# Reading the weight stream of an f32 transformer kernel two 1 MB blocks per transfer

## The reference

```
mod = silu(c) @ ada_w + ada_b            # 2048 -> 6144: shift, scale, gate
h   = rmsnorm(x) * (1 + scale) + shift
u   = h @ w_in                           # 2048 -> 16 heads q, k, v, z; 32 heads q, k, v, z; two gates
o_a = gated_delta_rule(silu(conv(qkv_a)), g, beta)      # 16 heads, chunks of 64
o_b = swa_with_sinks(rope(q_b), rope(k_b), v_b)         # 32 query heads, window 128
y   = sigmoid(g_a) * (o_a @ proj_a) + sigmoid(g_b) * (o_b @ proj_b)
x   = x + gate * (y @ w_out)
# third layer: neighborhood attention, a two-way linear recurrence, a gated feed-forward
# (2048 -> 5632 -> 2048), and a gated embedding product, each with its norms
```

## Time and profile before

| | |
|---|---|
| median of 3 executions | 4971.2 us (4965.88 to 4974.19) |
| the profiled execution | 4966.8 us, span 4965.0 us |
| TensorE busy | 4319.7 us, 87% of the span |
| VectorE busy | 2718.9 us, 55% |
| ScalarE busy | 2001.3 us, 40% |
| GpSimd busy | 222.4 us, 4% |
| HBM read | 752.64 MB, 152 GB/s over the span |
| mean granted TensorE clock | 0.927 |

### The profile page before, as it was taken

The page is one execution under the profiler, slowest core; times in us unless marked ns, Lnnn a source line. Parts: engine busy times, 40 slices in busy tenths (PEclk is TensorE's granted clock), DMA queues, the critical chain, the costliest instruction groups (busy, mean ns, idle before and its releaser), DMA issues.

```text
span 4965.0 us, 85375 instructions
## 1 busy us (share of the span) xinstructions
PE 4319.7 (87%) x33128; PEld 4146.8 (84%) x33128; DVE 2718.9 (55%) x3528; ACT 2001.3 (40%) x2916; POOL 222.4 (4%) x188
## 2 busy tenths in 40 slices
PE   2989898899979989898979997998996799999968
PEld 2888787799869988887869986997895799999958
DVE  7455655465657645556546565764345454555444
ACT  2333434244433434334324343334345444444443
POOL 0011111000000001111110000000000000000000
PEclk8999999699989989999969998998998899999979
DMA  8422222274348733222217532873332344444522
GB/s 352 141 97 103 98 103 102 93 279 153 122 147 298 247 110 120 97 101 98 105 54 264 203 119 101 298 257 136 112 138 85 127 166 174 171 176 173 186 96 102
DMA packets 117707, 757.57 MB, mean 153 GB/s; under 512 B 13008, under 2 KB 13328, under 8 KB 35600
## 3 DMA queue, kind: packets, MB, share of 16 engines
q1 hardware_dynamic: 87984, 639.17, 35.5%
q10 hardware_dynamic: 29536, 115.68, 6.7%
HBM read 752.64 MB, written 2.16 MB: 152 GB/s over the span
## 4 chain that ended last, share of the span: by engine, by line
PE 73%; DVE 9%; ACT 7%; issue 6%; DMA 2%; ACTq 1%; DVEq 1%; POOL 0%; SPq 0%; POOLq 0%
PE bank L275 17%; PE bank L276 17%; PE bank L277 17%; PE bank L779 2%; PE bank L740 2%; PE bank L1728 1%; PE bank L1730 1%; PE bank L1729 1%; PE bank L783 1%; DVE Wl L291 1%; DMA raw<-in_ada 1%; DVE WS L531 1%; PE bank L728 1%; ACT Wh L285 1%; PE bank L757 1%
## 5 line engine op out<-in xcount | busy, mean ns | idle before, releaser
L275 PE MATMUL bank<-Hh,Wh 128*128 128x256 f32 x7232 | 2129.8, 294 | 92.9 <-DVE Hl L410 34.4
L285 ACT CAST Wh<-raw 128x1024 fp32r<-128x1024 f32 x1140 | 1186.8, 1047 | 2332.5 <-PE bank L277 1875.0
L276 PE MATMUL bank<-Hl,Wh 128*128 128x256 f32 x7232 | 2067.9, 286 | 0.0
L277 PE MATMUL bank<-Hh,Wl 128*128 128x256 f32 x7232 | 2065.5, 286 | 0.0
L291 DVE TENSOR_TENSOR Wl<-raw,Wh 128x1024 fp32r<-128x1024 f32 x1140 | 1390.1, 1229 | 1214.1 <-ACT Wh L285 1211.4
L275 PEld LDWEIGHTS bank<-Hh,Wh 128*128 128x128 f32 x7232 | 1411.9, 195 | 139.5 <-issue 88.9
L276 PEld LDWEIGHTS bank<-Hl,Wh 128*128 128x128 f32 x7232 | 1411.9, 195 | 13.2 <-issue 12.6
L277 PEld LDWEIGHTS bank<-Hh,Wl 128*128 128x128 f32 x7232 | 1408.8, 195 | 0.0
L275 PE MATMUL bank<-Oh,Wh 128*128 128x256 f32 x1024 | 289.8, 283 | 0.0
L276 PE MATMUL bank<-Ol,Wh 128*128 128x256 f32 x1024 | 289.8, 283 | 0.0
L277 PE MATMUL bank<-Oh,Wl 128*128 128x256 f32 x1024 | 289.7, 283 | 0.0
(11 more groups left out here) (311 smaller groups left out, 4818.5 us busy)
## 6 DMA issues: line engine op xcount, KB each, us to landing
raw<-in_stream SPq DMA_DIRECT2D x572, 1024.0 KB, 4.8
gm_more<-in_ada ACTq DMA_DIRECT2D x80, 512.0 KB, 5.2
raw<-in_ada SPq DMA_DIRECT2D x32, 1024.0 KB, 7.5
WS<-in_ada ACTq DMA_DIRECT2D x48, 512.0 KB, 4.6
WS<-in_ada ACTq DMA_DIRECT2D x16, 1024.0 KB, 4.9
gm_more<-in_ada ACTq DMA_DIRECT2D x16, 1024.0 KB, 8.1
WS<-rows_d ACTq DMA_DIRECT2D x16, 512.0 KB, 5.9
X<-in_x_t SPq DMA_DIRECT2D x1, 2048.0 KB, 17.0
```

The costliest lines, as they stand in the source:

```text
L275: pe.matmul(out[:, 0:T], wh, xh[:, kt, :], start=first, stop=False)
L276: pe.matmul(out[:, 0:T], wh, xl[:, kt, :], start=False, stop=False)
L277: mm = pe.matmul(out[:, 0:T], wl, xh[:, kt, :], start=False, stop=last)
L285: act.copy(Wh[:, n % 4, :], raw[:, (sbk + 2) % 4, k * (D // 2):(k + 1) * (D // 2)]).then_inc(hi_ready, 1)
```

## The change

A read now fetches two neighbouring blocks into two neighbouring slots (2 MB), and there is one semaphore for each pair of slots. The read of blocks b and b+1 waits for what the read of block b+1 alone waited for. In the loop it is `lo_ready` of at least 2b-4; at the start it is the `ada` slab that freed the second slot. The casts of both blocks wait for the pair's semaphore. The number of reads falls from 572 to 286.

```diff
-        landed = [sem(f"raw{i}_landed") for i in range(4)]
+        landed = [sem(f"raw_pair{i}_landed") for i in range(2)]
...
         def act_cast(act, q, sbk, k):
 
             n = 2 * sbk + 4 + k
-            act.wait_ge(landed[(sbk + 2) % 4], (q + ((sbk + 2) // 4 + 1)) * 16)
+            act.wait_ge(landed[(sbk + 2) % 4 // 2], (q + ((sbk + 2) // 4 + 1)) * 16)
...
-            for s in range(4):
-                sp.wait_ge(ada_used, 2 * KT - 3 + s)
-                sp.dma_start(raw[:, s, :], stream[s]).then_inc(landed[s], 16)
+            for s in range(0, 4, 2):
+                sp.wait_ge(ada_used, 2 * KT - 2 + s)
+                sp.dma_start(raw[:, s:s + 2, :], stream[s:s + 2].rearrange("b p d -> p b d")).then_inc(landed[s // 2], 16)
             with sp.Fori(1, N_Q if until is None else until) as q:
-                for s in range(4):
-
-                    sp.wait_ge(lo_ready, q * 8 + (2 * s - 6))
-                    sp.dma_start(raw[:, s, :], stream[q * 4 + s]).then_inc(landed[s], 16)
+                for s in range(0, 4, 2):
+
+                    sp.wait_ge(lo_ready, q * 8 + (2 * s - 4))
+                    sp.dma_start(raw[:, s:s + 2, :], stream[bass.ds(q * 4 + s, 2)].rearrange("b p d -> p b d")).then_inc(landed[s // 2], 16)
...
             for n in range(4):
-                act.wait_ge(landed[n // 2], 16)
+                act.wait_ge(landed[0], 16)
                 act.copy(Wh[:, n, :], raw[:, n // 2, (n % 2) * (D // 2):(n % 2 + 1) * (D // 2)]).then_inc(hi_ready, 1)
```

## The result

In eight runs each the kernel before took 4969.44 us in the median (4958.39 to 4974.19) and the changed kernel 4990.09 us (4981.49 to 4993.16). The ratio is 1.0043, with a 95% interval of 1.0032 to 1.0054. The change costs 20.7 us, twice what I had called the smallest difference that can be told from none. The time lies inside the predicted range of 4965 to 4992 us. The likeliest case was wrong in size: it had 5.0 us, a quarter of the loss.

What follows compares the result with a forecast made beforehand. TensorE was taken to bound the kernel (73% of the chain, DMA 2%), with the weight stream hidden. All terms were 0 except 5.0 us for exposed decay rows: 4971.2 + 5.0 = 4976.2 us, range 4965 to 4992 us.

Steps and rivals of the forecast that it cites:

- Duration of a pair: Weight stream: a 2 MB read lands 7.3 us after its issue, bounds 4.8 and 7.6 us.
- Later issue, dense stages: Feed-forward, tightest place: a pair has 8.3 us and needs 7.3; casts have some 6.3 us more cover; cost 0.
- The start: First four casts run from 97.3 us, before VectorE wants them at 102.15; cost 0, with 3.8 us of cover.
- Fewer issues and semaphores: SyncE's queue: 286 issues of 0.33 us disappear, but that queue only waits; gain 0.
- The decay rows, exposed: Last delta-rule pass of both hybrid layers: rows stand behind one more megabyte, 2 x 2.5 = 5.0 us, bounds 0 to 5.6.
- Decay rows in the 14 other passes: Other delta-rule passes: the same 2.5 us delay, hidden by 5.0 us of cover; cost 0.
- slabs of half 0: `end`, half 0: second slab has only 0.4 us to spare but is issued before the 2 MB read; cost 0.
- The slabs of `end`, half 1: `end`, half 1: third slab has 3.6 us, a second megabyte takes 2.5, 1.1 us is left; cost 0.
- A: Decay rows get their turn after a read's first megabyte, so the change costs nothing: 4971.2 us; chance 0.27.
- B: `end`, half 1: late third slab holds up L531, 1.4 us in each of 16 rounds, about 4998 us; chance 0.13.
- C: Larger transfers pay, shortening the 0.99 us gap in 16 rounds of `end`, half 1: 4955 us; chance 0.07.
- D: Weight stream: the 2 MB read is much slower than 7.6 us, reaching TensorE in the feed-forward at 14.6 us; chance 0.03.

Runs made afterwards that it cites:

- run twelve: The changed kernel with each pair read another half block later: 5003.52 us, ratio 1.0072 against the kernel before.
- run two: The kernel before, 1 MB reads at their old times, but one semaphore for each pair of slots: 4966.98 us, ratio 0.9997.
- run one: The kernel before with the first block of a pair held until the second may go, two 1 MB reads back to back: 4992.06 us, ratio 1.005.
- all three edits: The kernel before (single reads) with casts before slabs, read held behind the decay rows, TensorE's feed-forward loop written out: 4928.14 us, ratio 0.9926.
- run six: The changed kernel with ScalarE's casts ahead of the slab issues in `end`, half 1: 4966.39 us, ratio 0.9999 against the kernel before.
- run four: Single reads in the two hybrid layers, 2 MB pairs in the third layer only: 4973.76 us, ratio 1.0017 against the kernel before.
- runs ten and nine: Casts before slabs, read behind decay rows, feed-forward loop written out: on the changed kernel's pairs 4929.82 us, on the kernel before's single reads 4928.14 us.

## Why the prediction was right and wrong

By the signs that the prediction itself gave for being wrong, two came: one cast waited for `raw`, and a dense stage, the feed-forward, changed.

**Duration of a pair**: 7.3 us taken, 7.6 us measured. The upper bound was the value.

**Later issue, dense stages, cost 0.** Right for the reads and their casts: the one wait of 1.8 us cost TensorE nothing, and run twelve shows 3.0 us of the cover. Wrong for the stage. The step went from "the casts are covered" to "the stage costs nothing", and forgot that TensorE's own code is fetched beside the stream. 13.7 us of such gaps stood in the trace of before, 10.6 of them under "issue". I had asked what a read pushes back in ScalarE's queue and left out the code queue. Cost: 4.3 us in gaps and some 1.6 us of clock.

**The start, cost 0.** Right. The pair's first cast starts at 97.78 us where it was 97.31, and VectorE's subtractions begin at 102.59, behind other work.

**Fewer issues and semaphores, 0.** Right: run two for the semaphore, and for the issues run one, where 572 reads end within 2 us of 286.

**The decay rows, exposed, 5.0 us.** The mechanism and the place were right and the term was undersized: 6.4 us (2.3 in the first layer, 4.1 in the second), above its upper bound of 5.6. The bound assumed that only the second megabyte is added. The queue rows show more: between 863.9 and 866.4 us of the changed kernel,

```profile
q1 hardware_dynamic: 115, 0.94, 89.0%
q10 hardware_dynamic: 61, 0.12, 13.1%
```

and in the same window before,

```profile
q10 hardware_dynamic: 272, 0.52, 60.6%
q1 hardware_dynamic: 42, 0.21, 20.4%
```

The decay rows do begin at the same time, near 863.9, but beside the pair they get 0.12 MB where they got 0.52. They get one packet for two of the stream (61 and 115), but theirs are a quarter of the size, 2 KB against 8. If the queues take turns by packets, that gives them little for as long as the stream has packets left. Why the second layer's pass lost 4.1 us and not 2.3 stays open.

**Decay rows in the 14 other passes, 0**, and **slabs of half 0, 0.** Right. In half 0 the slabs take 8.0 to 8.6 us and have 0.4 to 1.0 us to spare, as before, the first of each layer apart, which lands earlier. In the 14 passes TensorE's waits before L762 changed by 1.1 us in all (103.5 to 104.6).

**The slabs of `end`, half 1, 0.** The argument followed the slab to its landing, and there it held: the third slab had 3.6 us and still has 1.8. But a slab is also an instruction on ScalarE. The step named the casts that stand uncovered behind it and did not ask what the issue itself may cost. It costs 0.41 us in the round shown, 4.4 us in 14 rounds.

**The rivals.** A is refuted. Its rule did show itself in part: the Trainium skill (DMA: Bandwidth & Descriptors, Queues, rings and completion order) has the engines go round the queues, and the decay rows do get packets while the pair still moves. What fails is the price of 0 that I had worked out, 8.3 us to landing against 5.9. B had the right stage and the right consequence, uncovered casts, with the wrong cause: L531 never waited. Its 27 us needed a slab late by 5 us. C is refuted; the gap that it hoped to shorten grew, and it comes in 14 rounds, not in the 16 that B and C were priced with. D did not happen. I gave "slower by over 0.2%" 0.16, almost all of it for B. The sum of small terms that each stood at 0 had no chance of its own, and that is what came: 6.4 + 4.4 + 4.3 in gaps, and up to 6.6 of clock, which the sum did not have at all. So it is luck that the time lies inside the range. The upper end had been put at 4992 us for smaller versions of B, and no slab came late.

## What to carry to other kernels

Before merging or bunching transfers, list everything that uses the same DMA engines and is waited for without cover: small transfers in other queues, the DMA issue instructions in front of work that an engine needs, and the code that an engine fetches at a loop jump. Each is worth between 0.4 and 4 us each time it comes, and in a kernel whose main stream is well hidden they are all the difference there is. And where such a place is found, mending it may bring more than the change under study: here casts ahead of the issues brought 22.5 us, and all three edits 38.6.

## What the runs showed of the hardware

- A DMA issue on ScalarE is not of fixed length. It took 0.34 us as a rule. For the second of three slabs it took 0.54 to 0.78 us in 14 of 16 rounds, 6.2 us after a pair was asked for and 1.1 to 1.5 us before it landed. Two megabytes in two transfers did the same (run one, 0.61 to 0.77 us). Slabs issued 2.6 us after a pair took 0.34 us, and with the casts moved ahead of the slabs (run six) all took 0.34 us.
- Jumping back in TensorE's feed-forward loop costs 3.1 to 3.5 us of gap, 3.9 to 4.1 with a pair of blocks queued (up to 4.6 in run four). TensorE then runs at 1.2 GHz for a while, 17.1 us in all for the four jumps of the changed kernel. With the four jumps written out the stage was 25.5 us shorter, and then took 742.2 us with pairs and 742.1 us with single reads (runs ten and nine).
- A 2 MB read takes 7.6 us to land where 1 MB takes 4.8. A half-megabyte transfer issued 0.46 us behind it lands after 8.3 us, where it was 6.0 behind 1 MB; while both queues moved data it had one packet for two of the stream's.
